# Gate and branch products by tokens, 512 moving columns, with the gate bias added on VectorE

## What is computed

```python
y = jnp.einsum('bsnc,ncd->bsnd', br, w_branch[l])               # four products, 256 -> 1024
g = jax.nn.sigmoid(h @ w_gate[l] + b_gate[l]).reshape(B, S, N_BRANCH, D)   # 1024 -> 4096
x = x + jnp.sum(g * y, axis=2) @ w_o[l]
```

## Time and profile before

| | us |
|---|---|
| median of the runs | 831.43 |
| the profiled execution | 832.6 |
| its span, first to last instruction | 830.8 |
| TensorE (PE) busy | 816.9 (98%) |
| weight loads (PEld) busy | 749.1 (90%) |
| VectorE (DVE) busy | 544.4 (66%) |
| ScalarE (ACT) busy | 409.6 (49%) |
| GpSimd (POOL) busy | 45.7 (5%) |
| share of the DMA engines in the main queue | 52.1% |

### The profile page before, as it was taken

One profiled execution on the slowest core, in us unless ns is written; L12 is line 12 of the kernel. 1 busy time (PEld: TensorE's weight loads), 2 busy tenths in 40 slices (PEclk: granted clock), 3 DMA queues, 4 the chain that ended last, 5 costly groups with the idle time before them and its releaser, 6 DMA issues.

```text
span 830.8 us, 14799 instructions
## 1 busy us (share of the span) xinstructions
PE 816.9 (98%) x5763; PEld 749.1 (90%) x5763; DVE 544.4 (66%) x805; ACT 409.6 (49%) x698; POOL 45.7 (5%) x81
## 2 busy tenths in 40 slices
PE   7999999999999999999999999999999999999996
PEld 6999979999899999999899999799988999999995
DVE  6687676865776665555767675687665865555663
ACT  6356655655454444333464475575545544333442
POOL 1420000000010000000013100000000100000000
PEclk9999999999999999999999999999999999999999
DMA  8976534536347555566546755334353665566541
GB/s 248 227 233 198 158 120 135 150 105 204 101 156 237 169 174 178 200 202 199 170 128 194 241 167 177 116 102 153 126 177 104 212 199 178 197 202 198 170 137 50
DMA packets 100851, 141.09 MB, mean 170 GB/s; under 512 B 4797, under 2 KB 87041, under 8 KB 100801
## 3 DMA queue, kind: packets, MB, share of 16 engines
q1 hardware_dynamic: 99296, 137.12, 52.1%
q0 software_dynamic: 1216, 3.17, 1.7%
q10 hardware_dynamic: 288, 0.11, 0.1%
HBM read 139.33 MB, written 1.05 MB: 169 GB/s over the span
## 4 chain that ended last, share of the span: by engine, by line
PE 93%; DVE 3%; ACT 1%; issue 1%; POOL 1%; DMA 1%; POOLq 0%; ACTq 0%; DVEq 0%
PE bank_w L1190 20%; PE bank_w L1192 19%; PE bank_w L1191 19%; PE bank_acc L1190 8%; PE bank_acc L1191 8%; PE bank_acc L1192 8%; PE bank_acc L1286 2%; PE bank_o L1315 2%; PE bank_acc L1298 2%; DVE w_lo L810 2%; DMA cst<-in_table 1%; PE bank_x L1263 0%; PE bank_x L1268 0%; POOL rstd L498 0%; PE bank_x L1259 0%
## 5 line engine op out<-in xcount | busy, mean ns | idle before, releaser
L810 DVE TENSOR_TENSOR w_lo<-raw,w_hi 128x1024 fp32r<-128x1024 f32 (+1 forms) x256 | 309.0, 1255 | 49.6 <-ACT w_hi L575 49.5
L1190 PE MATMUL bank_w<-act_hi,w_hi 128*128 128x256 f32 x1008 | 287.9, 286 | 0.0
L1192 PE MATMUL bank_w<-act_hi,w_lo 128*128 128x256 f32 x1008 | 285.8, 283 | 0.0
L1191 PE MATMUL bank_w<-act_lo,w_hi 128*128 128x256 f32 x1008 | 285.2, 283 | 0.0
L575 ACT ACTIVATE w_hi<-raw 128x1024 fp32r<-128x1024 f32 (+1 forms) x256 | 257.0, 1060 | 26.7 <-DMA raw<-in_w_gate 12.9
L1190 PEld LDWEIGHTS bank_w<-act_hi,w_hi 128*128 128x128 f32 x1008 | 191.6, 190 | 6.9 <-ACT big L696 3.5
L1191 PEld LDWEIGHTS bank_w<-act_lo,w_hi 128*128 128x128 f32 x1008 | 190.9, 189 | 1.8 <-issue 0.5
L1192 PEld LDWEIGHTS bank_w<-act_hi,w_lo 128*128 128x128 f32 x1008 | 191.2, 190 | 0.0
L704 ACT ACTIVATE part_hi<-big 128x512 fp32r<-128x512 f32 x32 | 20.3, 633 | 194.2 <-DVE big L1038 191.5
L1190 PE MATMUL bank_acc<-w_hi,part_hi 128*128 128x512 f32 x256 | 100.3, 392 | 0.0
L1191 PE MATMUL bank_acc<-w_lo,part_hi 128*128 128x512 f32 x256 | 100.3, 392 | 0.0
(11 more groups left out here) (180 smaller groups left out, 938.5 us busy)
## 6 DMA issues: line engine op xcount, KB each, us to landing
raw<-in_w_ff SPq DMA_DIRECT2D x128, 512.0 KB, 4.7
raw<-in_w_gate SPq DMA_DIRECT2D x64, 512.0 KB, 4.7
raw<-in_w_in SPq DMA_DIRECT2D x32, 536.0 KB, 5.5
raw<-in_w_o SPq DMA_DIRECT2D x16, 512.0 KB, 4.5
raw<-in_w_branch SPq DMA_DIRECT2D x16, 256.0 KB, 4.5
raw<-in_w_branch SPq DMA_DIRECT2D x8, 512.0 KB, 4.6
xs<-in_x SPq DMA_DIRECT2D x2, 512.0 KB, 4.6
out_y<-big SPq DMA_DIRECT2D x4, 256.0 KB, 2.1
```

The source lines that it names most:

```text
L810: nc.vector.tensor_tensor(half_view(w_lo, c, hf), raw_half(c, hf), f32(half_view(w_hi, c, hf)), ALU.subtract).then_inc(w_lo_ready, 1)
L1190: nc.tensor.matmul(dst, s_hi, m_hi, start=first, stop=False)
L1191: nc.tensor.matmul(dst, s_hi, m_lo, start=False, stop=False)
L1192: ins = nc.tensor.matmul(dst, s_lo, m_hi, start=False, stop=last)
```

## The change

- A pair of gate chunks now holds 512 columns: the first chunk has the first half of the contraction, the second chunk the other half. TensorE works by tokens: in the first step of a pair it makes the product of tokens 0 to 127 with all 1024 of the contraction, so with both chunks, and in the second step that of tokens 128 to 255. The activations are the stationary side, 512 columns of the weights move: 2 x 4 x 3 = 24 matmuls of 512 columns a step. The first chunk is given back in the middle of the second step.
- The branch quarters are 6 matmuls of 512 columns, by tokens as well. The branch chunks y0, y1 and y2 stand after gate chunks 7, 9 and 13.
- The bias of a gate is now along the columns. GpSimd loads it as a row broadcast to all partitions (`gate_row`, 256 KB, eight a layer), VectorE adds it from PSUM into `big` (`gate_add`) at the start of the next step, and this frees the bank. ScalarE's tanh is then in place in `big`, one instruction of 512 columns, behind the splits of the next step.
- In the steps with `exps`, ScalarE empties the small job behind the product before it does the splits. On VectorE the quarters of a branch stand before and behind `maxima`, and all of them ahead of `normalise`.
- `mix` has tokens on the partitions now, so TensorE transposes it (`turn_mix`, 16 transposes a layer) before it is split.
- The small jobs uq0, uq1, ukv0, ukv1, dq1 and dk1 move by a place to one step.

```diff
-Y_AFTER = {3 * n + 6: n for n in range(NB - 1)}
+Y_AFTER = {7: 0, 9: 1, 13: 2}
+GROUPS = GATE_N // 2
...
-    "lq": (11, 1), "lkv": (12, 1), "uq0": (15, 0), "uq1": (15, 1), "ukv0": (16, 0), "ukv1": (16, 1),
-    "dq0": (18, 1), "dk0": (19, 0), "dq1": (19, 1), "dk1": (20, 0),
+    "lq": (11, 1), "lkv": (12, 1), "uq0": (15, 1), "uq1": (16, 0), "ukv0": (16, 1), "ukv1": (17, 0),
+    "dq0": (18, 1), "dk0": (19, 0), "dq1": (20, 1), "dk1": (21, 1),
...
 ScalarE:
             def gate(i, l):
-                act.wait_ge(w_used, used_count(l, POS["gate", i]))
-                if i >= 8:
-                    act.wait_ge(y_read, l * 16 + (i - 7))
-                bank = bank_w[:, W_AT["gate", i, 0] % 2, :]
-                for d in range(2):
-                    ins = nc.scalar.activation(big[:, i % 8, d * SEQ:(d + 1) * SEQ], bank[:, d * SEQ:(d + 1) * SEQ],
-                                               ACT.Tanh, bias=vec(BG + 2 * i + d, l), scale=0.5)
-                ins.then_inc(gate_tanh, 1)
+                g, t = divmod(i, 2)
+                z = gate_slot(g // 2, 2 * t + g % 2)
+                act.wait_ge(gate_read, l * GATE_N + (i + 1))
+                nc.scalar.activation(z, z, ACT.Tanh, scale=0.5).then_inc(gate_tanh, 1)
...
+                    if pair_heads(SOFTMAX, s):
+                        evac((s, 1), l)
                     for c in SPLIT_AT[s]:
                         split_hi(c, l)
-                    if kind == "gate":
-                        gate(j, l)
-                    evac((s, 1), l)
+                    if s > IN_N and CHUNKS[s - 1][0] == "gate":
+                        gate(CHUNKS[s - 1][1], l)
+                    if not pair_heads(SOFTMAX, s):
+                        evac((s, 1), l)
...
 VectorE:
+            def gate_add(i, l):
+                g, t = divmod(i, 2)
+                if t == 0:
+                    dve.wait_ge(gate_row_landed[g % 2], 16 * (l * GROUPS // 2 + g // 2 + 1))
+                    dve.wait_ge(gate_first, l * GROUPS + (g + 1))
+                else:
+                    dve.wait_ge(w_used, used_count(l, POS["gate", i]))
+                nc.vector.tensor_tensor(gate_slot(g // 2, 2 * t + g % 2), bank_w[:, t, :], gate_row[:, g % 2, :],
+                                        ALU.add).then_inc(gate_read, 1)
...
+                    if s > IN_N and CHUNKS[s - 1][0] == "gate":
+                        gate_add(CHUNKS[s - 1][1], l)
+                    if kind == "y" and j < NB - 1:
+                        branch(j, l, (0, 1))
                     for i in pair_heads(SOFTMAX, s):
                         maxima(i, l)
                     for i in pair_heads(HEAD_OUT, s):
                         heads_lo(i, l)
                     if kind == "y" and j < NB - 1:
-                        branch(j, l, (0, 1))
+                        branch(j, l, (2, 3))
...
 TensorE:
             def gate(i, l):
+                g, t = divmod(i, 2)
+                tok = slice(t * P, (t + 1) * P)
+                bank_free(("gate", g, t), l)
+                for half in range(2):
+                    c = POS["gate", 2 * g + half]
+                    hi, lo = k_view(w_hi, c, KD // 2), k_view(w_lo, c, KD // 2)
+                    if t == 0:
+                        pe.wait_ge(w_lo_ready, lo_count(l, c))
+                    sides = [(act_hi[:, half * KD // 2 + k, tok], act_lo[:, half * KD // 2 + k, tok], hi[:, k, :], lo[:, k, :])
+                             for k in range(KD // 2)]
+                    ins = split_product(bank_w[:, t, :], sides, half == 0, half == 1)
+                    if t == 1:
+                        ins.then_inc(w_used, 1)
+                if t == 0:
+                    ins.then_inc(gate_first, 1)
...
+            def turn_mix(q, l):
+                pe.wait_ge(mixed, l * 12 + (8 + q + 1))
+                for j in range(KD // 2):
+                    ins = nc.tensor.transpose(mix_banks[q][:, j * P:(j + 1) * P], mix[:, q, j * P:(j + 1) * P], ident)
+                ins.then_inc(mix_turned, 1)
+
+            def last_branch(l):
+                for q in range(3):
+                    branch_part(NB - 1, q, l)
+                turn_mix(0, l)
+                branch_part(NB - 1, 3, l)
+                turn_mix(1, l)
```

More of the change, by code:

```diff
@@ L75 @@
 W_JOBS = []
[L76 to L79, removed]
+for _g in range(GROUPS):
+    W_JOBS += [("gate", _g, t) for t in range(T)]
+    if 2 * _g + 1 in Y_AFTER:
+        W_JOBS += [("y", Y_AFTER[2 * _g + 1], q) for q in range(4)]
 W_JOBS += [("y", NB - 1, q) for q in range(4)]
@@ L315, in trunk_kernel @@
         x_evac = sem("x_evac")
+        gate_row_landed = [sem(f"gate_row_landed{b}") for b in range(2)]
+        gate_first = sem("gate_first")
+        gate_read = sem("gate_read")
         gate_tanh = sem("gate_tanh")
@@ L416, in load_half @@
                 dst = raw_half(c, h)
-                if kind in ("in", "gate", "f1"):
-                    w, n = {"in": (w_in, IN_C), "gate": (w_gate, 256), "f1": (w_ff1, 256)}[kind]
+                if kind == "gate":
+                    k = KD // 2 * (i % 2) + 2 * h
+                    src = w_gate.rearrange("l (k p) (c n) -> l c p k n", p=P, n=512)[l, i // 2]
+                    sp.dma_start(dst.rearrange("p (k n) -> p k n", k=2), src[:, k:k + 2, :]).then_inc(done, 16)
+                elif kind in ("in", "f1"):
+                    w, n = {"in": (w_in, IN_C), "f1": (w_ff1, 256)}[kind]
                     src = w.rearrange("l (k p) (c n) -> l c p k n", p=P, n=n)[bass.ds(l, 1), bass.ds(i + 2 * g, 1)]
@@ L509, in _ @@
                 norm(2 * l, l)
+                pool.wait_ge(gate_read, l * GATE_N)
+                for g in range(2):
+                    gate_bias(l, g)
                 uq = d_w_uq[bass.ds(l, 1)].rearrange("o k n -> (o k) n")
@@ L545, in _ @@
                              inv_rank[:, :, :].rearrange("p t h -> p (t h)"), l).then_inc(rs_d_ready, 1)
+                for g in range(2, GROUPS):
+                    pool.wait_ge(gate_read, l * GATE_N + 2 * (g - 1))
+                    gate_bias(l, g)
                 norm(2 * l + 1, l)
@@ L557, in _ @@
             act.wait_ge(rows_clear, 1)
-            for v, at, n in ((norm1_g, G1, KD), (norm2_g, G2, KD), (b_gate, BG, NB * KD)):
+            for v, at, n in ((norm1_g, G1, KD), (norm2_g, G2, KD)):
                 rows = vec_rows[DEPTH * at:DEPTH * (at + n), :]
@@ L739, in _ @@
                         in_evac(j, l)
+                    if pair_heads(SOFTMAX, s):
+                        evac((s, 1), l)
                     for c in SPLIT_AT[s]:
                         split_hi(c, l)
-                    if kind == "gate":
-                        gate(j, l)
-                    evac((s, 1), l)
[L746 to L749, removed]
+                    if s > IN_N and CHUNKS[s - 1][0] == "gate":
+                        gate(CHUNKS[s - 1][1], l)
+                    if not pair_heads(SOFTMAX, s):
+                        evac((s, 1), l)
+                mix_hi(0, l)
+                mix_hi(1, l)
                 split_hi(POS["o", 3], l)
+                mix_hi(2, l)
+                mix_hi(3, l)
                 k = 2 * l + 1
@@ L1054, in _ @@
             dve.wait_ge(rows_turned, 1)
[L1055 to L1058, removed]
+            nc.vector.tensor_copy(vec_all[:, :], bank_acc[:, 2, 0:DEPTH * NCOL]).then_inc(vec_ready, 1)
             dve.wait_ge(vec_ready, 1)
@@ new lines, in gate, with branch_part @@
+                if t == 0:
+                    ins.then_inc(gate_first, 1)
+            def branch_part(n, q, l):
+                c, (t, m) = POS["y", n], divmod(q, 2)
+                tok, cols = slice(t * P, (t + 1) * P), slice(m * 512, (m + 1) * 512)
+                hi, lo = k_view(w_hi, c, 2), k_view(w_lo, c, 2)
+                if q == 0:
+                    pe.wait_ge(w_lo_ready, lo_count(l, c))
+                    pe.wait_ge(o_lo_ready, l * (NH // 2) + (2 * n + 2))
+                bank_free(("y", n, q), l)
+                sides = [(part_hi[:, n % 2, k, tok], part_lo[:, n % 2, k, tok], hi[:, k, cols], lo[:, k, cols]) for k in range(2)]
+                split_product(bank_w[:, W_AT["y", n, q] % 2, :], sides, True, True).then_inc(y_done if q < 3 else w_used, 1)
@@ L1525, in _ @@
                         gate(j, l)
-                    if kind == "y":
+                    if kind == "y" and j < NB - 1:
                         branch(j, l)
```

64 lines of the change are left out of this document (34 added, 30 removed).

## The result

The changed kernel took **838.27 us** (median, 837.67 to 839.34), the kernel before in the same series 831.35 (831.16 to 832.05): ratio 1.0083, 95% interval 1.0067 to 1.0099, so 6.9 us more. The forecast was 834.4: right in sign, and 3 to 4 us short in size. The time lies inside the stated range of 826 to 840 and outside the 832.9 to 837 of the forecast case.

The account below looks back on a forecast made before the run. The prediction took TensorE's own stream plus its waits as the bound (93% of the last chain). Its terms summed to +3.0 us, giving 834.4 us on the median, range 826 to 840; the forecast case, chance 0.50, had 832.9 to 837.

Parts of the forecast that it names:

- wide matmuls: Gates and branches: one 512-column matmul saves 10.3 ns over two of 256; -9.9 us over 40 chunks.
- transposes of mix: Sixteen new transposes a layer on TensorE's own stream, with nothing to hide them; +3.5 us.
- y0: Step 16: second quarter waits 2.1 us a layer for gate 7's addition, behind ScalarE's emptying, split and normalise; +4.2 us.
- y1: Step 19: gate 10 waits 1.4 us a layer for quarter 2's bank, read only after both heads' maxima; +2.8 us.
- y2: Step 24: TensorE waits 0.3 us a layer for a bank freed behind step 23's split and normalise; +0.6 us.
- turn_prob of step 10: Waits for normalise, delayed by gate 0's addition and cq's emptying, with TensorE coming earlier; +1.2 us.
- y3 and the tail: Step 27's split delays the last tanh and y3's reading, then w_o waits for the first mix tile; +0.6 us.
- Rival 3: Wide matmuls save less, 7.0 instead of 9.9 us, at the slower distance of 232.3 ns; 837.3 us, chance 0.10.
- rival 1: VectorE and ScalarE keep up, so no bank waits at y0, y1 or elsewhere; 825.0 us, faster, chance 0.16.
- rival 2: One of the two long waits, at y0 or y1, is hidden; about 831 us, chance 0.17.
- rival 4: A pair's second chunk comes late at step 8 or behind a later load; 836 to 839 us, chance 0.07.
- The distance and the three waits: Gate matmuls start 228 to 232 ns apart; TensorE waits in y0's second quarter, before gate 10, and in y3.

Follow-up runs that it names:

- e4: e3 with each 512-column matmul of gates and branches issued as two of 256 columns; 835.50 us, 1.0039 of the kernel before, 6.8 us more than e3.
- e5: e3 with the 16 transposes of mix a layer issued twice each; 831.58 us, 0.9992 of the kernel before, 2.85 us more than e3.
- e7: The changed kernel with ScalarE's split ahead of the emptying of uq0 in step 15; 834.37 us, 1.0020 of the kernel before.
- e2: The changed kernel with one head's maxima ahead of y1's first two quarters in step 19; 835.44 us, 1.0040 of the kernel before.
- e10: The changed kernel with gate 1's addition ahead of step 9's split and gate 13's between split and normalise in step 23; 835.23 us, 1.0035 of the kernel before.
- e3: The changed kernel with e2's and e10's orders, gate 7's addition ahead of step 15's split, last tanh ahead of ScalarE's step 27 split; 828.46 us, 0.9956 of before.
- e6: e3 with bias rows loaded for the first two groups of each layer only, 12 of 16 transfers left out; 828.49 us, 0.9958 of the kernel before.
- e8: e3 with e7's order of step 15 as well; 827.28 us, 0.9939 of the kernel before, the fastest.

## Why the prediction was right in sign and short in size

| term, us for both layers | predicted | measured | by |
|---|---|---|---|
| wide matmuls | -9.9 (-10.8 to -7.0) | -6.8 (to -7.3) | e4, its timeline |
| transposes of mix | +3.5 | +3.4 (2.85 timed) | e5 and the covered wait |
| y0 | +4.2 | +3.9 to 4.3 | timeline, e7 |
| y1 | +2.8 | +2.8 | e2 |
| y2 | +0.6 | +1.0 | landmarks of e10 |
| turn_prob of step 10 | +1.2 | none | waits |
| gate 1's addition, step 11 | not seen | +1.6 | landmarks of e3 |
| y3 and the tail, against before | +0.6 | about +0.3 | timelines |
| sum | +3.0 | +6.2 to 6.6; with -7.3, +5.7 to 6.1 | |
| change of the time | +3.0 | +6.0 and +6.9 | two series |

**The step that failed is the size of the wide matmuls**: 2.6 to 3.1 us too much was credited to them, and 3.0 to 3.9 were missing from the time. The other errors are small beside it or cancel: y2 was 0.4 short, y3 0.3 too long, and step 10's 1.2 was missing where step 11's 1.6 was not foreseen. I took 229.3 ns for 512 columns as the mean of the MLP's run and w_o's, and 119.8 ns for 256 columns from one step. The MLP's second product has the same operand roles as w_o (activations stationary, weights moving), so roles are not what parts 228.3 from 230.2, and what does stays open. But the trace of before had the better figures. Over its unbroken distances the mean is 230.8 ns in w_o (178 distances) and 228.6 in the MLP (736), and it is 119.3 ns for the gates and branches (some 1800). 2 x 119.3 - 230.8 = 7.8 ns, not 10.3. After the change the gates and branches have 230.9 ns (some 860), so w_o's was the one to take. Each pair is a small difference of two large numbers, and 960 pairs make 1 us of each nanosecond.

Rival 3, with 10% of the chance, named this term, and its time of 837.3 came nearest. That is partly luck: it asked for 232.3 ns, and the distance was 230.9. Of the 2.5 ns by which a pair saved less, 1.5 lie on the side of 512 columns and 1.0 on that of 256, where nothing in the prediction doubted the 119.8.

**Lateness at y0, y1 and y2** came as walked: 1.96 and 1.42 us a layer measured, 2.1 and 1.4 predicted, and the same instruction named. Both rival 1 and rival 2 fall: both waits are in the trace, and e7 and e2 take them away by order alone. y2 (0.20 in the row, 0.5 on TensorE) was short for the break's own price.

**Step 10 was the wrong job in the right place.** I expected `normalise` of step 9 to be late by 1.9 us. It came 0.3 us later against turn_prob in layer 0 (80.61 and 80.83 after; 81.11 and 81.62 before) and 1.2 in layer 1, inside the slack. In layer 0 VectorE was ahead, since the half of chunk 11 that its list waits for landed 1.58 us earlier (split by ScalarE from 67.68, before from 69.26); why it landed earlier no run shows. The wait is near: in e4 it did show in layer 0, where the loads for turn_prob waited 0.45 and 0.30 us for `normalise`. But I stopped at the first user. The addition of gate 1 stands behind `normalise` and `d_norm`, and gate 3 wants its bank 0.8 us after turn_prob begins. The wait that I priced at 1.2 us was there at 1.6 for another job.

**y3 and the tail.** A quarter of y3 late by the addition of gate 15 (0.29), the next by VectorE's multiply (0.43 + 0.11) and w_o's wait for the first tile (0.28) make 1.1 us a layer, for 0.95 before: 0.72 in y3 and 0.23 in w_o, whose run was broken once for `act_lo` of the later tiles. The forecast had 1.3 for 1.0, and did not see the first of the three.

**What was counted as hidden is hidden**: the bias rows (e6, 0.2 us) and the second chunk of a pair at step 8 (rival 4: between 60 and 215 us and between 470 and 625, the two mixing stages, TensorE's matmuls have no wait for `w_lo`; the load in front of y2 has one, and its matmul isn't late by it). My argument against rival 4 was misread, though: the earlier trace rows name no releaser, and ScalarE's splits of those halves do wait for landings. This is the timeline of before:

```profile
60.88 1.06 ACT L575 ACTIVATE w_hi<-raw 128x1024 fp32r<-128x1024 f32 x1 [0.89 <-DMA raw<-in_w_gate]
```

**The signs.** The distance and the three waits came as written. The stretch from the first gate to the end of y3 did not stay about the same in layer 0: it grew from 151.1 to 152.5 us.

**Check of the whole.** Before's 832.5, less 6.8 for the wide matmuls, plus 3.4 for the transposes, less what e8's tail saves against before's, 2 x (0.95 - 0.57), is 828.3. With 7.3 for the wide matmuls it is 827.8. e8 took 827.28, nearer to the second, and the rest is within its interval. What remains between the two series for the same kernel (1.0072 and 1.0083, 0.9 us) is within their intervals too, and I leave it open.

## What to carry to other kernels

When an edit moves the reading of a bank to another engine or a step later, walk that engine's list in its fixed order from the last thing that it waits for on TensorE, through every user of every bank behind it, and not to the first one only; a busy share of 66% says nothing on this, since VectorE was idle for 6 us right ahead of the wait that it caused. In a list, put what waits for the end of TensorE's step behind what doesn't. Where a term is a small difference times a thousand instructions, take the mean of all distances on both sides of it, each from the stage nearest to the one that changes, and don't average stages: one nanosecond is then a microsecond. And price an added instruction with what it will cover: doubling it can hide in a wait that the first one made.

## What the runs showed of the hardware

- A break in a run of 512-column matmuls costs some 0.27 us beyond PE's row of waiting: e8 gained 1.2 us by its timelines (0.61 and 0.63 a layer) where e3's rows showed 0.6. A break of 0.29 us in y3 has no row in PE's list at all, only one among the weight loads.
- In these split products, where every matmul has its own weight load, matmuls start 119.3 ns apart for 256 columns with weights stationary (before), 119.1 to 119.2 with activations stationary (e4), and 230.5 to 230.9 for 512 in the gates and branches: going from 256 to 512 columns gained 3.3% of these matmuls' time.
- The same matmul with the same operand roles has another distance in another stage: 230.8 ns in w_o and 228.6 in the MLP's second product, in the trace of before. No run shows why.
- The same four transposes cost 0.43 us when doubled between two runs of matmuls and 0.16 in front of w_o's first matmul, which waited for VectorE beside them: what an instruction on TensorE's own stream costs depends on the wait that it can cover.
